# A Mixture-of-Experts block in float32 on one core: the expert biases as rounded part plus remainder, added by one rounded-format product

## What is computed

```python
def clamped_swiglu(g, u):
    g = jnp.minimum(g, SWIGLU_LIMIT)
    u = jnp.clip(u, -SWIGLU_LIMIT, SWIGLU_LIMIT)
    return g * jax.nn.sigmoid(SWIGLU_ALPHA * g) * (u + 1)

    # moe(): tokens sorted by expert into blocks, then for each block
    def expert_block(args):
        xb, e = args
        hid = xb @ w1[e] + b1[e]
        return clamped_swiglu(hid[:, :D_FF], hid[:, D_FF:]) @ w2[e] + b2[e]
...
    contrib = ys[dest] * gate_sorted[:, None]
    return jax.ops.segment_sum(contrib, tok_sorted, num_segments=T)
```

## Time and profile before

| | |
|---|---|
| median of 3 runs | 1585.44 us (1583.59 to 1587.69) |
| the profiled execution | 1581.37 us, span 1579.6 us |
| busy: PE, DVE, ACT | 1460.2 us (92%), 501.9 us (32%), 304.1 us (19%) |
| mean granted TensorE clock | 0.948 of full speed |
| read from HBM | 497.98 MB, 316 GB/s over the span |

### The profile page before, as it was taken

How to read it: one execution, slowest core, us unless ns; L and a number is a source line. 1 busy time by engine, 2 the same in 40 slices (tenths; PEclk the granted TensorE clock), 3 DMA queues, 4 the chain that set the end, 5 groups by cost and what they waited for, 6 DMA issues and landing times.

```text
span 1579.6 us, 17439 instructions
## 1 busy us (share of the span) xinstructions
PE 1460.2 (92%) x6832; PEld 764.6 (48%) x6832; DVE 501.9 (32%) x896; ACT 304.1 (19%) x445; POOL 15.5 (1%) x34
## 2 busy tenths in 40 slices
PE   4997987999999999999999999999999778899996
PEld 2774455433333433434334334334333557799975
DVE  1645434112212112212212211211121556655564
ACT  3414222001001101101001001001011344444441
POOL 1000001000000000000000000000000000000000
PEclk8999997999999999999999999998999877899998
DMA  9217905799999999999999999999998531455530
GB/s 377 103 34 332 403 27 189 306 423 427 429 429 427 429 427 428 427 428 417 424 426 416 425 428 414 425 428 379 429 424 374 183 104 63 151 187 187 187 107 27
DMA packets 62615, 499.57 MB, mean 316 GB/s; under 512 B 6200, under 2 KB 22616, under 8 KB 34896
## 3 DMA queue, kind: packets, MB, share of 16 engines
q1 hardware_dynamic: 59472, 492.85, 76.2%
q0 software_dynamic: 1648, 5.04, 1.0%
q10 hardware_dynamic: 1456, 1.16, 0.2%
HBM read 497.98 MB, written 1.05 MB: 316 GB/s over the span
## 4 chain that ended last, share of the span: by engine, by line
PE 70%; DMA 13%; DVE 10%; issue 3%; ACT 2%; SPq 1%; PEldq 0%; DVEq 0%; ACTq 0%
PE bank L1400 25%; PE bank L547 21%; PE bank L583 14%; DMA ring<-in_w 12%; PE bank L557 4%; PE bank L592 2%; DMA ring<-in_w_ada 2%; PE bank L603 1%; DVE dk L665 1%; DVE mrows L669 1%; DVE w_lo L410 1%; DVE dk L659 1%; PE bank L565 1%; ACT xn L839 1%; PE bank L1696 0%
## 5 line engine op out<-in xcount | busy, mean ns | idle before, releaser
L547 PE MATMUL bank<-ring,xn 128*64 128x512 f32 x2048 | 468.9, 616 | 20.4 <-DMA ring<-in_w 19.0
L547 PEld LDWEIGHTS bank<-ring,xn 128*64 128x64 f32 x2048 | 155.8, 141 | 330.4 <-issue 330.3
L583 PE MATMUL bank<-ring,dq 128*64 128x512 f32 x1024 | 226.8, 595 | 0.0
L654 DVE TENSOR_SCALAR mrows<-bank 128x512 f32<-128x512 f32 x32 | 20.6, 686 | 484.2 <-PE bank L547 484.2
L625 ACT ACTIVATE sq<-mrows 128x512 f32<-128x512 f32 x32 | 19.6, 630 | 792.9 <-DVE mrows L654 792.9
L583 PEld LDWEIGHTS bank<-ring,dq 128*64 128x64 f32 x1024 | 70.6, 137 | 142.8 <-issue 140.1
L410 DVE TENSOR_TENSOR w_lo<-ring,w_hi 128x2048 fp32r<-128x2048 f32 (+1 forms) x48 | 103.2, 2158 | 41.3 <-ACT w_hi L403 41.0
L678 DVE TENSOR_TENSOR dk<-bank,bc 128x512 f32<-128x512 f32 x32 | 22.1, 691 | 256.2 <-PE bank L583 256.2
L403 ACT ACTIVATE w_hi<-ring 128x2048 fp32r<-128x2048 f32 (+1 forms) x48 | 85.9, 1802 | 32.4 <-PE bank L1400 32.2
L1400 PE MATMUL bank<-x_hi,w_hi 128*128 128x256 f32 x256 | 73.2, 286 | 1.8 <-DVE h_lo L1278 1.8
L1400 PE MATMUL bank<-h_lo,w_hi 128*128 128x256 f32 x256 | 73.1, 286 | 0.0
(11 more groups left out here) (331 smaller groups left out, 1496.9 us busy)
## 6 DMA issues: line engine op xcount, KB each, us to landing
ring<-in_w SPq DMA_DIRECT2D x192, 2048.0 KB, 16.3
ring<-in_w_ff SPq DMA_DIRECT2D x32, 1024.0 KB, 5.3
ring<-in_w_ada SPq DMA_DIRECT2D x24, 1024.0 KB, 16.0
ring<-in_w_out SPq DMA_DIRECT2D x8, 1024.0 KB, 8.7
ring<-in_w_in SPq DMA_DIRECT2D x8, 992.0 KB, 26.2
ring<-in_w_in SPq DMA_DIRECT2D x8, 640.0 KB, 8.3
ring<-in_w_ple_gate SPq DMA_DIRECT2D x4, 1024.0 KB, 4.7
xc<-in_ctx SPq DMA_DIRECT2D x1, 1024.0 KB, 5.1
```

Of the source, the lines that this page charges most:

```text
L547: m = pe.matmul(banks[bank_no][mine(i), :], gathered[:, k, mine(i)], rows_of(at + i, 2)[:, k % 2, q * 512:(q + 1) * 512], start=k == 0, st ...
L583: m = pe.matmul(banks[OUT_BANKS[c]][mine(i), :], actT[:, k, mine(i)], rows_of(8 + 2 * j + i, 4)[:, r, c * 512:(c + 1) * 512], start=k == 0 ...
L654: dve.tensor_scalar(gs[:, half * 512:half * 512 + 512], banks[GATE_BANKS[half]][:], LIMIT, None, ALU.min)\
```

## The change

The two bias rows of a pair are loaded twice, into partitions 0 and 1 and into partitions 32 and 33 of a zeroed tile (`b1raw`, `b2raw`). ACT writes the rounded values of all 34 partitions into `b1rows` and `b2rows`; DVE overwrites partitions 32 and 33 with the remainder, raw minus rounded. `pick_rows` has its two rows of ones at partitions 0, 1 and again at 32, 33, so that one product in the rounded format, with a contraction of 34, adds rounded part and remainder. All four loads of a pair now stand at the start of ACT's pair. The semaphores around the square roots are merged into two (`ms_done`, `root_done`), with the counts adjusted.

```diff
@@ tiles
-        b2rows = xc[0:2, 0, :]
-        b1rows = dv[0:2, :, :].rearrange("p t c -> p (t c)")
-        pick = small[0:2, :]
+        b1raw = hT[0:34, 0:4, :].rearrange("p k c -> p (k c)")
+        b2raw = dqT[0:34, :, :].rearrange("p h t -> p (h t)")
+        pick_rows = over("pick_rows", [34, P], "csig")
+        b1rows = over("b1rows", [34, 2 * FF], "dv")
+        b2rows = over("b2rows", [34, D], "xc")
@@ hidden
-                    pe.wait_ge(moe("b1_in", which), (n + 1) * 16)
+                    pe.wait_ge(moe("bias_split", which), n * 2 + 2)
                     for q, bank_no in enumerate(GATE_BANKS + UP_BANKS):
-                        m = pe.matmul(banks[bank_no][:], pick, b1rows[:, q * 512:(q + 1) * 512],
+                        m = pe.matmul(banks[bank_no][:], pick_rows[:].bitcast(F32R),
+                                      b1rows[:, q * 512:(q + 1) * 512].bitcast(F32R),
                                       start=False, stop=False, skip_group_check=True)
@@ pe_rest
-                    pe.wait_ge(moe("b2_in", which), (n + 1) * 16)
+                    pe.wait_ge(moe("bias_split", which), n * 2 + 3)
                     for c in range(2):
-                        pe.matmul(banks[OUT_BANKS[c]][:], pick, b2rows[:, c * 512:(c + 1) * 512],
+                        pe.matmul(banks[OUT_BANKS[c]][:], pick_rows[:].bitcast(F32R),
+                                  b2rows[:, c * 512:(c + 1) * 512].bitcast(F32R),
                                   start=False, stop=False, skip_group_check=True)
...
-        def load_b1(act, n, pair, which):
-            act.dma_start(b1rows, a["b1"][0, bass.ds(pair * 2, 2), :]).then_inc(moe("b1_in", which), 16)
-        def load_b2(act, n, pair, which):
-            act.dma_start(b2rows, a["b2"][0, bass.ds(pair * 2, 2), :]).then_inc(moe("b2_in", which), 16)
+        def load_biases(act, n, pair, which):
+            act.wait_ge(moe("bias_split", which), n * 2 + 1)
+            for rows in (slice(0, 2), slice(32, 34)):
+                act.dma_start(b1raw[rows, :], a["b1"][0, bass.ds(pair * 2, 2), :]).then_inc(moe("bias_in", which), 16)
+                act.dma_start(b2raw[rows, :], a["b2"][0, bass.ds(pair * 2, 2), :]).then_inc(moe("bias_in", which), 16)
+        def round_b1(act, n, which):
+            act.wait_ge(moe("bias_in", which), (n + 1) * 64)
+            act.activation(b1rows[:].bitcast(F32R), b1raw, ACT.Copy).then_inc(moe("bias_rounded", which), 1)
+        def round_b2(act, n, which):
+            act.activation(b2rows[:].bitcast(F32R), b2raw, ACT.Copy).then_inc(moe("bias_rounded", which), 1)
+        def rest_of_b1(dve, n, which):
+            dve.wait_ge(moe("bias_rounded", which), n * 2 + 1)
+            dve.tensor_tensor(b1rows[32:34, :].bitcast(F32R), b1raw[32:34, :], b1rows[32:34, :], ALU.subtract)\
+                .then_inc(moe("bias_split", which), 1)
+        def rest_of_b2(dve, n, which):
+            dve.wait_ge(moe("bias_rounded", which), n * 2 + 2)
+            dve.tensor_tensor(b2rows[32:34, :].bitcast(F32R), b2raw[32:34, :], b2rows[32:34, :], ALU.subtract)\
+                .then_inc(moe("bias_split", which), 1)
@@ dve_pair
             m.then_inc(moe("selg_ready", which), 1)
+            rest_of_b1(dve, n, which)
...
+            rest_of_b2(dve, n, which)
             for c in range(2):
@@ POOL, ahead of the loop
-            step(pool.memset(pick, 1.0))
...
+            step(pool.memset(small[0:34, :], 0.0))
+            for at in (0, 32):
+                pick = small[at:at + 2, :]
...
+            step(pool.memset(b1raw, 0.0), wait=False)
+            step(pool.memset(b2raw, 0.0), "raw_zero")
@@ ACT, the loop
             with act.Fori(0, PAIRS) as pair:
-                load_b1(act, pair, pair, MAIN)
+                load_biases(act, pair, pair, MAIN)
+                round_b1(act, pair, MAIN)
                 sigmoids(act, pair, MAIN)
                 gather_out(act, pair + 1, MAIN)
-                load_b2(act, pair, pair, MAIN)
+                round_b2(act, pair, MAIN)
                 act_rest(act, pair, MAIN)
@@ DVE, ahead of the loop
+            dve.wait_ge(sem("pick_done"), 2)
+            step(V.tensor_copy(pick_rows[:].bitcast(F32R), small[0:34, :]), "pick_copied")
+            dve.wait_ge(sem("raw_zero"), 1)
```

More of the change, by code:

```diff
@@ L729, in _ @@
             step(pool.iota(iota_i, pattern=[[1, CAP]], base=0, channel_multiplier=0), "iota_done")
-            step(pool.memset(pick, 1.0))
[L732 to L735, removed]
+            step(pool.memset(small[0:34, :], 0.0))
+            for at in (0, 32):
+                pick = small[at:at + 2, :]
+                step(pool.memset(pick, 1.0))
+                step(pool.affine_select(out=pick, in_=pick, compare_op=ALU.is_gt, fill=0.0, base=1,
+                                        pattern=[[1, P]], channel_multiplier=-CAP))
+                step(pool.affine_select(out=pick, in_=pick, compare_op=ALU.is_gt, fill=0.0, base=CAP,
+                                        pattern=[[-1, P]], channel_multiplier=CAP), "pick_done")
+            step(pool.memset(b1raw, 0.0), wait=False)
+            step(pool.memset(b2raw, 0.0), "raw_zero")
             pool.wait_ge(sem("hf_done"), 2 * NT)
@@ L803, in _ @@
                 if t == 2:
-                    act.wait_ge(sem("lat_ms"), 1)
-                    step(act.activation(stat[:, 24:30], stat[:, 18:24], ACT.Sqrt), "lat_root")
+                    act.wait_ge(sem("ms_done"), 2)
+                    step(act.activation(stat[:, 24:30], stat[:, 18:24], ACT.Sqrt), "root_done")
                 if t < 2:
@@ L846, in _ @@
                 elif u == 9:
-                    act.wait_ge(sem("sub_ms"), 1)
-                    step(act.activation(stat[:, 48:56], stat[:, 40:48], ACT.Sqrt), "sub_root")
+                    act.wait_ge(sem("ms_done"), 3)
+                    step(act.activation(stat[:, 48:56], stat[:, 40:48], ACT.Sqrt), "root_done")
             for j in (2, 3):
@@ L856, in _ @@
             step(act.activation(xn[:, 0, :], xc[:, 2, :], ACT.Square, accum_out=stat[:, 0:1]), "ss2_done")
-            act.wait_ge(sem("ms2_done"), 1)
-            step(act.activation(stat[:, 4:5], stat[:, 2:3], ACT.Sqrt), "root2_done")
+            act.wait_ge(sem("ms_done"), 4)
+            step(act.activation(stat[:, 4:5], stat[:, 2:3], ACT.Sqrt), "root_done")
             def feed_forward_turned(t):
@@ L869, in _ @@
                                     accum_out=stat[:, 8 + n:9 + n]), "ss2_done")
-            act.wait_ge(sem("ms2_done"), 2)
-            step(act.activation(stat[:, 5:6], stat[:, 3:4], ACT.Sqrt), "root2_done")
+            act.wait_ge(sem("ms_done"), 5)
+            step(act.activation(stat[:, 5:6], stat[:, 3:4], ACT.Sqrt), "root_done")
             feed_forward_turned(1)
@@ L887, in _ @@
             with act.If(most_act > CAP):
+                act.wait_ge(moe("bias_split", MAIN), 2 * PAIRS + 1)
                 with act.Fori(1, ROUNDS) as r:
@@ L891, in _ @@
                             n = (r - 1) * PAIRS + pair
-                            load_b1(act, n, pair, OVER)
+                            load_biases(act, n, pair, OVER)
                             gather_out(act, n, OVER)
+                            round_b1(act, n, OVER)
                             sigmoids(act, n, OVER)
-                            load_b2(act, n, pair, OVER)
+                            round_b2(act, n, OVER)
                             act_rest(act, n, OVER)
@@ L905, in _ @@
             step(act.activation(xn[:, 0, :], x2[:, 0, :], ACT.Square, accum_out=stat[:, 0:1]), "ss3_done")
-            act.wait_ge(sem("ms3_done"), 1)
-            step(act.activation(stat[:, 4:6], stat[:, 2:4], ACT.Sqrt), "root3_done")
+            act.wait_ge(sem("ms_done"), 6)
+            step(act.activation(stat[:, 4:6], stat[:, 2:4], ACT.Sqrt), "root_done")
             def transposed(name, dst, k, scale=1.0):
@@ L951, in _ @@
             for t in range(NT):
-                act.wait_ge(sem("var1"), t + 1)
-                step(act.activation(stat[:, 16 + t:17 + t], stat[:, 12 + t:13 + t], ACT.Sqrt), "root4_done")
+                act.wait_ge(sem("ms_done"), 7 + t)
+                step(act.activation(stat[:, 16 + t:17 + t], stat[:, 12 + t:13 + t], ACT.Sqrt), "root_done")
                 if t == 0:
@@ L975, in _ @@
             for t in range(NT):
-                act.wait_ge(sem("var2"), t + 1)
-                step(act.activation(stat[:, 26 + t:27 + t], stat[:, 22 + t:23 + t], ACT.Sqrt), "root5_done")
+                act.wait_ge(sem("ms_done"), 9 + t)
+                step(act.activation(stat[:, 26 + t:27 + t], stat[:, 22 + t:23 + t], ACT.Sqrt), "root_done")
                 if t == 0:
@@ L1239, in _ @@
             step(V.tensor_copy(most_i[:], most[:, 0:1]), tile="rank")
-            dve.sem_inc(moe("y_added", MAIN), 1)
-            dve.sem_inc(moe("y_added", OVER), 1)
+            dve.wait_ge(sem("pick_done"), 2)
```

(19 more changed lines are left out.)

16 lines of the change are left out of this document (8 added, 8 removed).

## The result

| | before | with the change |
|---|---|---|
| median of 8 runs each | 1584.97 us (1582.08 to 1588.23) | 1594.83 us (1589.47 to 1599.52) |
| the profiled execution | 1581.37 us, span 1579.6 | 1595.18 us, span 1593.4 |

The ratio is 1.0058, with a 95% interval of 1.0040 to 1.0076: slower by 0.6%, some 9.9 us.

A forecast was written before the change was run, and what follows sets the result against it. Weight transfers were taken to bound the loop; 14.6 - 1.1 - 1.1 - 1.4 + 1.1 + 0.3 = +12.4 us gave 1593.8 us for the profiled execution and 1597.8 us for the median, range 1587 to 1604.

The forecast's parts named there:

- The transfers lead: Expert loop: weight-block transfers, not PE, set the pace to the loop's end, at 59.69 us per pair.
- Rival D: Expert loop: PE is the bound after all, so 53 us go, to 1533 us; chance 0.02.
- 0.97 us per pair for one set of loads: Loop's bias loads: the present two cost the weight stream this much, and doubling them adds 0.97 us more per pair.
- The 15 groups: Bias loads of pairs 1 to 15, ahead of block 5 of pair 15: 15 x 0.97 = +14.6 us there.
- Rival B: Loop's bias loads: the copies stand on other engines and cost the stream nothing, 1583.2 us; chance 0.10.
- C: Loop's bias loads: four loads in one burst interrupt once instead of twice, 1576 us; chance 0.06.
- two DMA engines that carry rows: Loop's bias loads: each of two engines carries 12 KB beside the ring, 0.46 us plus completions, delaying blocks.
- the lateness: Block 5 of pair 15: PE's lag behind the landing goes, -1.1 us.
- the products: Last pair's bias products on PE: the rounded format saves 1.1 us in the first layer, 1.4 in the second.
- ACT's rounding: Rounding b2 between ACT's two copies: +1.1 us per pair on PE's path, hidden except in the last pair.
- DVE, POOL and the work ahead of the loop: Before the loop: POOL's extra masks and zeroing hidden; DVE's added cast and hand-over delay all loads by +0.3 us.
- DVE's remainders: In the loop: the subtractions fall where DVE idles before its bank waits, costing nothing.

The follow-up runs named there:

- before_double: The kernel before with each bias load issued twice, the second copy into rows nothing reads, no rounding, float32 products: 1598.51 us, ratio 1.0109 to the kernel before.
- one_set: The changed kernel without the loads of rows 32 and 33, so two loads and 24 KB per pair: 1581.89 us against 1581.70 for the kernel before.
- short: The changed kernel with its four loads per pair cut to 128 bytes a row, most of each bias left out: 1569.41 us, ratio 0.9915 to the kernel before.
- spread16: The changed kernel with each row loaded by its own load in 16 pieces that can't be merged, same partitions: 1598.01 us, ratio 1.0090 to the kernel before.
- resident: The changed kernel with all 32 rows of both biases loaded once ahead of the loop, none inside it: 1564.04 us, ratio 0.9862 to the kernel before.
- other_port: The changed kernel with the second copy of the rows in partitions 64 and 65 instead of 32 and 33: 1589.02 us, ratio 1.0031 to the kernel before.
- spread: The changed kernel with each row loaded by its own load, eight per pair, the intended 16 pieces going as one: 1591.09 us, ratio 1.0071 to the kernel before.
- four_ways: The changed kernel with the rows in partitions 8 and 12 and the second copy in 72 and 76: 1586.77 us, ratio 1.0027 to the kernel before.

## Why the prediction was right

The forecast was 1597.8 us with 1587 to 1604, and 1593.8 for the profiled execution; measured were 1594.83 and 1595.18. Against before: +12.4 forecast, +9.9 by the medians.

- **The transfers lead.** Held in every run: from the landing of block 5 of pair 15 to the end (median less landing, with medians of several chips) it is 393 to 398 us in the eight kernels with rounded products and 398 to 402 us in the three with float32 ones, while the landings themselves lie 32 us apart. Rival D, the 53 us of PE, is out; PE got 4.0 us per pair faster and waits for longer.
- **0.97 us per pair for one set of loads, the same again for the second.** Measured 0.92 and 0.89, which before_double and one_set show from either side. The 15 groups gave +14.0 us at the landing (1197.7 against 1183.7), where 14.6 + 0.3 were forecast. Rival B had 59.7 us per pair, C less; neither came.
- **The reason given for it was wrong in two points.** The text put the cost on two DMA engines that carry rows and on their completions (0.46 us of bytes, the rest completions). short shows that completions cost nothing that can be seen (0.02 us per pair), and spread16 that spreading the rows over all engines doesn't help (2.10 us). That the price doubled was right by luck: loads, bytes, completions and bytes into the same partitions all double with the change, so each of them as the cause would have given the same forecast. A copy in partition 64 would have cost less than the forecast, and the text would not have said so.
- **PE behind that landing.** Forecast: -1.1 for the lateness, -1.1 and -1.4 for the products, +1.1 for ACT's rounding, in all -2.5. Measured: the scatter ends 42.0 us after the landing, where it was 1229.3 - 1183.7 = 45.6: **-3.6**. The other rounded kernels show the same (41.9 to 42.0 us with loads, 41.0 in resident), the float32 ones 44.5 to 45.6. Up to the work on block 7 the two first terms are near: that work began 10.0 us after the landing in place of 11.9, -1.9 for the -2.2 forecast. The second product gave -1.3 for -1.4, and ACT's rounding +0.8 for +1.1 (0.82 in the chain above). What the sum had at nothing, and only the range allowed for, is that the 32 records behind the first product took 7.02 us in place of 8.40. The granted clock shows where that went. Before, it stood at half its full level (1.2 in place of 2.4 GHz) from the bias products into those records; with the change it stood there ahead of the products, after PE's idle 2.71 us for block 5, where PE had time to spare before block 7:

```profile
1194.90:1198.30 3.40, 3.40 (x9) 0.92 (x10) 0.00 (x0) 0.00 (x0) 0.00 (x0) 0.50 1.02 436
```

```profile
1198.90:1202.20 3.30, 3.30 (x11) 1.10 (x9) 0.00 (x0) 0.00 (x0) 0.00 (x0) 0.50 1.04 442
```

  In other_port the clock is full there, PE waits for block 7 instead (it landed at 1203.2, 9.8 us after block 5), and the scatter ends at the same 42.0 us.
- **The end.** The scatter ends at 1239.7, where it was 1229.3, so +10.4 us; the first work behind the loop (DVE's square sum) starts at 1244.9, where it was 1234.9, so +10.0, near the medians' +9.9. The profiled execution's span grew by 13.8 us; its other 3.8 us fell behind the loop, where nothing is changed, and the runs' own spread is wider than that (1589.47 to 1599.52). So the profiled number, 1593.8 against 1595.18, is close by two misses of opposite sign: +12.4 us were forecast, +10.0 are there where the loop ends, and 3.8 that were not forecast lie behind it.
- **DVE, POOL and the work ahead of the loop**: the forecast was +0.3. PE began pair 0 at 279.91 us in place of 278.93, but from kernel to kernel that start lies anywhere between 277.56 and 281.77, so the term can't be read. In the loop DVE's remainders are hidden, as said. ACT waited 104.0 us in 16 pairs for the bias loads, 6.5 us each, inside its own idle time.

## What to carry to other kernels

Where the DMA engines are busy all the time, a load of a few rows is not priced by its share of the traffic: 24 KB a pair, a thousandth of it, held up all 25 MB by 1.6% (0.92 of 58.73 us). Before making an operation on TensorE cheaper by giving it more operand rows, ask how they come in: load small tables once, many rows at a time, ahead of the stream. And a forecast that comes out right doesn't prove the mechanism that was written beside it; here only the runs that took bytes, carriers and destinations apart showed where it was wrong.

## What the runs showed of the hardware that I had not expected

- Four loads of two rows cost 0.02 us per pair at 128 bytes a row and 1.81 at 8 and 4 KB. Four loads as such cost nothing that shows; their bytes do.
- Loss for 48 KB per pair: 1.81 us for two-row loads and 1.87 for one-row loads into partitions 0, 1, 32, 33; 2.10 for the same in 16 pieces each; 1.50 with the copy in 64 and 65; 1.36 in 8, 12, 72 and 76.
- The ring's own packets get longer beside the bias loads. This is in the traces' packet records, which the views only sum up. Between the landings of block 5 of pairs 2 and 15 a ring packet of 16 KB takes 0.61 us in the median of every kernel. In short and resident none takes over 0.65 us. With the change 38 a pair do, and are longer than the median by 12.4 us together (summed over the 16 engines), while all the pair's bias packets take only 2.05 us. The same sum is 7.5 us in the kernel before and 6.4 in one_set; with 48 KB it is 15.5 in before_double, 12.0 in spread, 12.2 in other_port, 12.8 in four_ways and 16.2 in spread16. It hardly falls where the loss does: other_port and four_ways have the change's sum at a smaller loss.
- **Open**: why ring packets get longer, and how carrying and entering add. If entering the partitions alone counted, the last two would be 0.9 and 0.5 us; if carrying alone did, spread16 would be 0.1. The same four loads lost 1.4 us even with their rows far apart. No run here separates the two further. The side of HBM was not varied: every kernel's loads in the loop read the same rows, the second set those of the first, and this too may hold up the stream.
- ACT's rounding of b2 takes 1.05 us on 34 partitions, as 128 partitions took 1.06.
